# A state-space scan whose output pieces and first raw products change places, and whose last output piece is issued in parts of 48 and 16 columns

## The reference, cut to what matters

```
u  = h @ in_w
bu = einsum('gnp,blgp->lbgn', b_bar, u)                # input of the states
states = associative_scan(s[l] = lam_bar*s[l-1] + bu[l])
y  = real(einsum('gpn,lbgn->blgp', cmat, states)) + d_skip*u
g  = gelu(y)
z  = g @ glu_w + glu_b ;  val, gate = split(z)
out = val * sigmoid(gate)
```

## Time and profile before

| what | value |
|---|---|
| median of 3 runs | 2447.71 us (2445.46 to 2448.32) |
| the profiled execution | 2444.28 us |
| its span | 2442.5 us |
| TensorE busy | 2392.6 us, 98% of the span |
| VectorE busy | 1863.1 us, 76% |
| ScalarE busy | 1039.8 us, 43% |
| mean granted TensorE clock | 0.998 of full |

### The profile page before, as it was taken

The page is one execution under the profiler, slowest core; times in us unless marked ns, Lnnn a source line. Parts: engine busy times, 40 slices in busy tenths (PEclk is TensorE's granted clock), DMA queues, the critical chain, the costliest instruction groups (busy, mean ns, idle before and its releaser), DMA issues.

```text
span 2442.5 us, 34094 instructions
## 1 busy us (share of the span) xinstructions
PE 2392.6 (98%) x12953; PEld 1925.4 (79%) x12953; DVE 1863.1 (76%) x3012; ACT 1039.8 (43%) x1241; POOL 35.3 (1%) x68
## 2 busy tenths in 40 slices
PE   8999999999999999999999999999999999999998
PEld 5585578778888888888878888788888888888886
DVE  8469989878888887888879987887777754455457
ACT  5353134454434444344454434556444344434442
POOL 0000000000000000000000000000000000000000
PEclk9999999999999999999999999999999999999999
DMA  9978859779989997898758877646798666666674
GB/s 376 399 255 317 336 193 319 237 250 340 309 286 310 340 305 263 291 338 297 246 174 292 277 261 221 190 143 197 252 302 282 219 193 188 191 190 193 193 222 140
DMA packets 313338, 630.58 MB, mean 258 GB/s; under 512 B 26740, under 2 KB 27156, under 8 KB 313176
## 3 DMA queue, kind: packets, MB, share of 16 engines
q1 hardware_dynamic: 307664, 613.36, 74.7%
q0 software_dynamic: 4288, 13.90, 2.1%
q10 hardware_dynamic: 1224, 1.14, 0.1%
HBM read 626.20 MB, written 2.11 MB: 257 GB/s over the span
## 4 chain that ended last, share of the span: by engine, by line
PE 87%; DVE 9%; issue 2%; ACT 1%; DMA 0%; SPq 0%; DVEq 0%; ACTq 0%
PE psB L2288 39%; PE psA L2288 39%; DVE prod L1533 2%; DVE tmp L1538 1%; DVE st L1544 1%; PE psT L1838 1%; PE psM L1870 1%; DVE ada_acc L1209 1%; DVE w_lo L1192 1%; PE psB L2095 1%; PE psT L2288 0%; PE psT L1902 0%; PE psT L2083 0%; PE psA L2060 0%; PE psM L1850 0%
## 5 line engine op out<-in xcount | busy, mean ns | idle before, releaser
L1192 DVE TENSOR_TENSOR w_lo<-w_raw,w_hi 128x1024 fp32r<-128x1024 f32 x728 | 888.0, 1223 | 459.0 <-ACT w_hi L838 454.7
L838 ACT ACTIVATE w_hi<-w_raw 128x1024 fp32r<-128x1024 f32 x728 | 770.5, 1060 | 1095.0 <-PE psB L2288 476.3
L2288 PE MATMUL psB<-w_hi,hT_hi 128*128 128x512 f32 x1040 | 407.1, 391 | 0.0
L2288 PE MATMUL psB<-w_hi,hT_lo 128*128 128x512 f32 x1040 | 404.9, 389 | 0.0
L2288 PE MATMUL psB<-w_lo,hT_hi 128*128 128x512 f32 x1040 | 404.7, 389 | 0.0
L2288 PE MATMUL psA<-w_hi,hT_hi 128*128 128x512 f32 x1008 | 397.6, 394 | 2.3 <-DVE w_lo L1192 2.0
L2288 PE MATMUL psA<-w_hi,hT_lo 128*128 128x512 f32 x1008 | 392.9, 390 | 0.0
L2288 PE MATMUL psA<-w_lo,hT_hi 128*128 128x512 f32 x1008 | 392.4, 389 | 0.0
L1209 DVE SCALAR_TENSOR_TENSOR ada_acc<-ada_raw,csil,ada_acc 128x512 f32<-128x512 f32 x465 | 347.5, 747 | 14.6 <-DVE ada_acc L1209 0.5
L2288 PEld LDWEIGHTS psB<-w_hi,hT_hi 128*128 128x128 f32 x1040 | 195.2, 188 | 45.7 <-issue 4.5
L2288 PEld LDWEIGHTS psA<-w_hi,hT_hi 128*128 128x128 f32 x1008 | 189.2, 188 | 49.1 <-issue 8.0
(11 more groups left out here) (402 smaller groups left out, 2368.4 us busy)
## 6 DMA issues: line engine op xcount, KB each, us to landing
w_raw<-in_ffn_w_in SPq DMA_DIRECT2D x352, 512.0 KB, 4.6
ada_raw<-in_ada_w SPq DMA_DIRECT2D x496, 256.0 KB, 5.5
w_raw<-in_ffn_w_out SPq DMA_DIRECT2D x176, 512.0 KB, 4.6
col_raw<-in_ada_w SPq DMA_DIRECT2D x128, 512.0 KB, 7.4
w_raw<-in_dsa_in_w SPq DMA_DIRECT2D x112, 512.0 KB, 4.6
w_raw<-in_s_glu_w SPq DMA_DIRECT2D x56, 512.0 KB, 5.5
w_raw<-in_s_in_w SPq DMA_DIRECT2D x32, 512.0 KB, 7.9
w_raw<-in_dsa_out_w SPq DMA_DIRECT2D x32, 512.0 KB, 5.4
```

The costliest lines, as they stand in the source:

```text
L838: nc.scalar.activation(high(u), w_raw[:, u % RING], ACT.Copy).then_inc(w_hi_ready, 1)
L1192: V.tensor_tensor(low(u), w_raw[:, u % RING], high(u).bitcast(F32), ALU.subtract).then_inc(w_lo_ready, 1)
L2288: ins = MM(PS[s][:, t, 0:r.width] if into is None else into, a_[:, kt, tok], b_[:, kk, 0:r.width], start=kt == begin and m == 0, stop=kt = ...
```

## The change

The four `units(2, 3)` ahead of piece 0 go away, and with them their empty matmuls. The column units keep their order; the four pairs that lose their place are used after raw units 0 and 2, behind piece 1 and within the inside products of piece 3. The raw units 0 to 3 of token half 0 are multiplied between pieces 0 and 1; SP issues their DMAs ahead of column unit 110 (`RAW_AT`). Piece 3 is issued twice: 48 columns (`SOONER`) of all eight f once chunk 111 of half 1 is stored, and 16 columns once all are; raw units 0, 1 and 2 of token half 1 stand between the two.

```diff
+FIRST_RAW = 4
+RAW_AT = FRONT + 46
+SOONER = 3 * HALF // 4
...
+                        if a == RAW_AT:
+                            sp.wait_ge(bu_full, 8)
+                            for k in range(FIRST_RAW):
+                                raw_unit(k)
                         col_unit(a)
-                    sp.wait_ge(bu_full, 8)
...
                         if whole(r, i, n // r.units):
-                            raw_unit(n)
+                            if n >= FIRST_RAW:
+                                raw_unit(n)
...
-            def outputs(n, f):
+            def outputs(n, f, first=0, end=HALF):
...
-                            ins = MM(outputs_place(n, f, d)[rows], Ctab[d][ri][:, f, rows], st[:, c0:c0 + HALF, half, g, ri, f % 8],
-                                     start=False, stop=f % 4 == 3 and d + ri == 2)
-                if f % 8 == 7:
+                            ins = MM(outputs_place(n, f, d)[rows, first:end], Ctab[d][ri][:, f, rows],
+                                     st[:, c0 + first:c0 + end, half, g, ri, f % 8],
+                                     start=False, stop=f % 4 == 3 and d + ri == 2 and end == HALF)
+                if f % 8 == 7 and end == HALF:
                     ins.then_inc(y_full, 1)
...
-                for n in range(4):
-                    units(2, 3)
-                for half in range(2):
-                    pe.wait_ge(rec, rec_after(half, HALF - 1))
-                    for f in range(8 * half, 8 * half + 8):
-                        outputs(half, f)
-                        if f % 2:
-                            units(2)
-                    if half == 0:
+                pe.wait_ge(rec, rec_after(0, HALF - 1))
+                for f in range(8):
+                    outputs(0, f)
+                    if f % 2:
                         units(2)
+                units(2)
+                for k in range(FIRST_RAW):
+                    whole_products(k, 0)
+                    if k % 2 == 0:
+                        units(2)
+                pe.wait_ge(rec, rec_after(1, HALF - 1))
+                for f in range(8, KT):
+                    outputs(1, f)
+                    if f % 2:
+                        units(2)
+                units(2)
                 pe.wait_ge(gelu_done, 2)
                 for f in range(8, KT):
                     ins = outputs_inside(3, f)
+                    if f == 11:
+                        units(2)
                 ins.then_inc(inside_done, 1)
-                for k in range(glu.units):
+                for k in range(FIRST_RAW, glu.units):
                     whole_products(k, 0)
...
                 early_products(glu.units - 1)
-                whole_products(0, 1).then_inc(w_used, 1)
+                pe.wait_ge(rec, rec_after(1, HALF + SOONER - 1))
+                for f in range(8, KT):
+                    outputs(3, f, 0, SOONER)
+                for k in range(FIRST_RAW - 1):
+                    whole_products(k, 1).then_inc(w_used, 1)
                 pe.wait_ge(rec, rec_after(1, CHUNKS - 1))
                 for f in range(8, KT):
-                    outputs(3, f)
-                for k in range(1, glu.units):
+                    outputs(3, f, SOONER)
+                for k in range(FIRST_RAW - 1, glu.units):
```

## The result

The changed kernel takes 2450.86 us (median of 18 runs, 2447.82 to 2455.89), the kernel before 2445.93 us (median of 18, 2444.44 to 2448.32). The ratio is 1.0021 with a 95% interval of 1.0014 to 1.0027: slower by about 5 us, at the bound of what can be told from no change. The profiled execution took 2454.14 us, 3.3 more than the median, so its stretches show the loss larger than the medians do.

What follows compares the result with a forecast made beforehand. TensorE was taken as the bound (98% busy, 87% of the chain). Duplicated pass +7.3, earlier piece 2 -3.4, vanished wait -0.33, together 3.6, kept as 3.4: 2447.71 + 3.4 = 2451.1 us; range 2447 to 2455.

Steps and rivals of the forecast that it cites:

- a short part of 16: Sign of being wrong: piece 3's last 16 columns taking clearly less than the forecast 7.3 us.
- a piece 2 well after 304 us: Sign of being wrong: TensorE reaching piece 2 well after 304 us; its start was forecast at 303.9.
- the queue ahead of it hides this: Front half: column unit 109, issued later than before, still lands at 250.3 us because transfers are queued ahead.
- the 1.3 of the sum: Front half: price of one column unit's transfer, 1.3 us, from pairs arriving every 2.6 us.
- Rival 1: Slower, 2453.5 us, chance 0.18: the stall at 253.3 us halves the granted clock, taking 1.7 us of work.
- the front half gains 3.4 us: TensorE is ready for piece 2 at 302.9, starts it at 303.9 instead of 307.3 us: 3.4 us stays.
- the spacing follows the width of the weights and not the columns: Piece 3's split: 28.6 ns a record whatever the columns, so 7.3 us for each part.
- the lower bound: Piece 3's split: a price in proportion to the columns, 5.5 us for 48 and 1.8 for 16.
- rival 2: Faster, 2443.8 us, chance 0.10: columns set the price, both parts cost 7.3 us together; decides below 11.2 us.
- the split had no wait to fill: Scan's end, before the change: TensorE ran until 318.29 us and the wait ended at 318.62, so hardly any wait.
- the shift passes on: Behind 338.6 us everything starts from TensorE's products, so the 3.4 us loss reaches the end.
- Rival 3: Loss taken up later, 2449 us, chance 0.07: VectorE-bound waits from 374 to 420 us leave 1.2 of 3.4 us.

Runs made afterwards that it cites:

- e4_between: The changed kernel with the four early raw transfers each issued in its place of use, split kept; 2448.56 against 2446.27 us before, ratio 1.0009.
- e3_fed: The changed kernel with empty matmuls, 28 before piece 0's wait and 96 before the pair with unit 110; 2452.31 us, ratio 1.0026 to the kernel before.
- e11_again: The changed kernel, unchanged, measured a second time; 2452.92 against 2446.73 us for the kernel before, ratio 1.0024.
- e2_front_only: The changed kernel with piece 3 whole again behind raw unit 0, as before; 2447.24 against 2446.27 us for the kernel before, ratio 1.0004.
- e1_split_only: The kernel before with only piece 3 split into 48 and 16 columns, raw units 0 to 2 between; 2449.75 against 2446.27 us, ratio 1.0016.
- e6_gap: The kernel before with the split alone, raw unit 2 moved into the middle of the part of 16; 2449.41 against 2446.08 us, ratio 1.0012.
- e5_between_whole: The changed kernel with early raw transfers in places of use and piece 3 whole behind raw units 0 to 2; 2442.56 against 2446.08 us before, ratio 0.9985.

## Why the prediction was right or wrong

**The total was near, its two largest terms were not.** Forecast were +3.4 us and 2451.1 us; the medians differ by 4.9 and the kernel takes 2450.86. That the absolute time came out within 0.3 us is luck twice over: errors of opposite sign, and a start of 2447.71 us (3 runs) that lies 1.8 above the 2445.93 of 18 runs. The prediction named two signs of being wrong, a short part of 16 and a piece 2 well after 304 us, and both came. The gates were forecast at 342.0 and came at 347.1 and 346.4 in the two profiles. The terms were off with opposite signs:

| from | forecast | after | difference |
|---|---|---|---|
| start of piece 2, earlier than 307.3 | 303.9 | 310.2 | +6.3 |
| start of piece 2 to start of the part of 48 | 9.1 | 9.1 | 0.0 |
| part of 48 and part of 16, start to start, with holes | 14.6 | 11.4 | -3.2 |
| end of the part of 16 to the gates | 9.1 | 11.0 | +1.9 |

These four make 5.0, which is what 347.1 has over 342.0 but for rounding and 0.05 us in the raw units between the parts.

**First failed step: "the queue ahead of it hides this".** Unit 109 was forecast to be issued late without harm. It was issued at 246.9 us and landed 3.8 us later, about half of the time of a unit behind a full queue: the queue had run nearly dry, as the DMA share of 0.72 from 246 to 248 us shows. The first raw unit left only at 247.3, and the four raw units landed between 253.6 and 258.9 instead of by 255.5. Units 110 and 111 came at 260.1 and 261.4 instead of 258.1. From the landing of unit 109 at 250.8 to that of unit 111 at 261.4 us, six transfers took 1.8 us each and not the 1.3 of the sum; that is 2.8 of the 3.3 us by which they came late. The stretches from 246 to 256 us moved 246, 282, 238, 323 and 369 GB/s; what they lack against 407 is worth 2.8 us too (an estimate from these rates). The mechanism, a stall behind four transfers put ahead of two that are needed first, was right, and `e4_between` shows it by taking it away. Its size was 6.8 us and not 4.8. (The price of 1.3 us was read from starts at 250.38 and 253.02 us, of which the second followed TensorE's outputs and not a landing; 512 KB at 407 GB/s give the same 1.3.)

**Rival 1 came in too.** The clock fell to 0.50 within the stall. From start to start the pair then took 2.1 us instead of 1.0 and the first raw unit 2.5 instead of 1.9 (the pair at 266.19 in this profile, the raw unit at 262.41 in `e3_fed`), 1.7 us in all, the 1.7 that the rival had; in `e11_again` the pair, the raw unit and the next pair together cost 3.0. The rival's source, the stretch at 1572 us, was idle for VectorE and "issue" and not for a transfer; the wait of 6.77 us here is the case that it was meant for. TensorE was ready for piece 2 at 310.2 us, 7.3 behind the 302.9 of the forecast: 3.4 by the later landings, 1.7 by the clock, 0.8 by small waits (0.48 for a column unit, 0.35 for `w_raw`), and the rest by pairs and raw units that each take about 0.1 us more than priced where they alternate. Only 1.0 of it was slack. So "the front half gains 3.4 us" became a loss of 2.9 in this execution and of 2.2 in `e2_front_only`.

**Second failed step: "the spacing follows the width of the weights and not the columns".** A record takes 9, 15, 23 and 28.6 ns at 16, 32, 48 and 64 strided columns. The one-column matmuls from which I inferred the contrary had weights of 128, four times as wide, and so said nothing of narrow ones. The rule of the Trainium skill that I set beside it (TensorE: Matmul & The Clock Gate, Back-to-back issue gap), one gap of about 25 ns between 1 and 64 columns, does not hold for these matmuls either: 9 ns a record, 18 ns for the two records of a matmul, is below it. The busy times of 6.0 and 2.6 us, tails included, lie near the lower bound (5.5 and 1.8). That rival 2 still did not come true is due to the holes, 1.1 and 1.9 us, a term that the prediction did not have: TensorE waiting for its own instructions. With them the parts cost 11.4 us, just over the 11.2 from which rival 2 decides. In `e1_split_only` they cost 10.6 against 7.3 whole, and that run is slower by 3.5 us.

**Right: the split had no wait to fill.** Before, TensorE waited 0.3 us for the last state. A second pass over eight f costs 3.1 us (`e3_fed`) to 4.7 us (`e11_again`), 4.1 in the profile after (1.6 in `e6_gap`), and the raw units between its parts would have been done anyway. `e5_between_whole` shows the same units filling the same time for nothing.

**Right: the shift passes on.** From the gates to the end of the span it takes 2103.9 us before, 2105.3 after, and between 2103.9 and 2105.9 in all experiments: never shorter than before. Rival 3 fell.

**Unforeseen.** Behind the hole of 1.93 us the clock fell again from 336 us, and the last units and the turned row took 1.9 us longer; in `e11_again` they took 9.3 us, near the 9.1 of the forecast. The front half's wait for VectorE before piece 2 did not exist, as TensorE came too late for it. The split alone (+0.16%) and the front alone (+0.04%) add up to about the whole (+0.21 and +0.24%).

**What stays open.** That the holes are waits for instructions is shown by the transfers on the instruction queue that end them and by `e6_gap`, where long matmuls in between nearly close one. What decides when such a transfer begins is not shown: it began from 2.3 us before the hole to 1.4 us after it had opened, and the hole ended 2.2 to 2.7 us behind its beginning. Why the gains of 1.6 us (`e6_gap`) and 3 us (`e3_fed`) in single profiles are not in the medians isn't known; holes vary from execution to execution, from 1.9 to 3.4 us for the same part of 16.

## What to carry to other kernels

Where one queue issues in order, put each transfer in the place of its use: four units ahead of the two needed first cost a stall of 6.8 us, and spread out they cost next to none; with that and the last piece whole, a loss of 0.2% became a gain of 0.15 to 0.2%. Before cutting a group of matmuls in parts so as to start it sooner, see whether TensorE waits there at all, and fill the time with whole pieces of work that need nothing late; a quarter of the columns cost 2.9 to 5.9 us here, where all of them cost 7.3. Where a profile says "issue", look for a transfer on the instruction queue just before the end of the hole. A price must be inferred from rows that have the same weights' width and the same stride as the operation in question.

## What the runs showed of the hardware

- The same matmul (32-wide weights, 64 moving columns, float32) takes 28.6 ns a record with columns 512 bytes apart and 15 ns with neighbouring ones.
- Short matmuls at 15 ns a record or less ran for some 200 to 250 records, and then came a hole of 1.0 to 3.4 us that no semaphore explains. At 23 to 30 ns a record holes came too, in some executions (0.2 to 2.3 us).
- Each of 33 such holes ended 1.2 to 1.6 us behind the landing of a 16 KB transfer on the profile's instruction queue (for instance landing at 331.43 and end at 332.72 us in `e1_split_only`).
- Idle time of 1.6 to 2 us was already followed by the low level of the clock for about 3 us (from 244 and from 336 us), which makes a hole of 1.93 us cost 3.8. It does not follow each time: behind the hole of 2.30 us in `e1_split_only`, and behind waits of 1.71 us (`e2_front_only`) and 1.94 us (`e4_between`) ahead of piece 0, the clock stayed at 1.00.
